# First norm's sum in a decoder trunk's expert stage: rows kept on chip, or spread by TensorE, with 20 or 22 initial expert places

## The reference

```python
x = _layer_norm(DEEPNORM_ALPHA * x + mixed, ln1_g[l], ln1_b[l])        # z * g + b
ffn = _hier_moe(x, ...)      # per expert e: silu(x Wg[e]) * (x Wu[e]), weighted, times Wd[e]
x = _layer_norm(DEEPNORM_ALPHA * x + ffn, ln2_g[l], ln2_b[l])
```

## Time and profile before

| | |
|---|---|
| median of 3 runs | 1338.53 us (1337.99 to 1340.18) |
| profiled execution, own time | 1340.83 us |
| its span, first to last instruction | 1338.6 us |
| busy share PE, DVE, ACT, POOL | 98%, 44%, 36%, 2% |
| TensorE clock granted, mean | 0.994 of full |
| DMA over the span | 364.95 MB, mean 273 GB/s |
| expert loads | 3 x 64 units of 1024 KB, median 21 to 23 us from issue to landing |

### The profile page before, as it was taken

How to read it: one execution, slowest core, us unless ns; L and a number is a source line. 1 busy time by engine, 2 the same in 40 slices (tenths; PEclk the granted TensorE clock), 3 DMA queues, 4 the chain that set the end, 5 groups by cost and what they waited for, 6 DMA issues and landing times.

```text
span 1338.6 us, 17749 instructions
## 1 busy us (share of the span) xinstructions
PE 1310.5 (98%) x7285; PEld 964.2 (72%) x7285; DVE 584.2 (44%) x757; ACT 483.3 (36%) x671; POOL 28.2 (2%) x49
## 2 busy tenths in 40 slices
PE   9999999999999999999999999999999999999994
PEld 9999989998888888888888888754444443544432
DVE  4387444446545655554555555515112121220206
ACT  4454444435465634454333433422111121211211
POOL 1000000400000000000100001000000000000000
PEclk9999999999999999999999999999999999999997
DMA  9767555545545445655566795799999999999995
GB/s 303 259 195 263 176 188 189 189 159 172 173 138 177 157 142 174 202 162 165 182 196 218 263 392 174 271 379 413 422 421 421 422 421 421 422 421 421 420 406 218
DMA packets 120461, 364.95 MB, mean 273 GB/s; under 512 B 11528, under 2 KB 17096, under 8 KB 96336
## 3 DMA queue, kind: packets, MB, share of 16 engines
q1 hardware_dynamic: 114080, 359.58, 72.3%
q10 hardware_dynamic: 6320, 4.49, 1.1%
HBM read 361.95 MB, written 2.10 MB: 272 GB/s over the span
## 4 chain that ended last, share of the span: by engine, by line
PE 91%; DMA 6%; DVE 2%; SPq 1%; ACT 0%; issue 0%; DVEq 0%
PE main L1127 19%; PE main L1129 19%; PE main L1128 19%; PE main L528 14%; PE att L599 7%; PE att L482 4%; DMA mraw<-in_expert_w_down_dram 3%; DMA mraw<-in_expert_w_up_dram 2%; PE att L1376 1%; DMA raw<-in_w_in_dram 1%; PE main L494 1%; PE main L495 1%; PE att L1359 1%; PE att L1395 1%; PE att L1391 1%; PE att L1346 0%
## 5 line engine op out<-in xcount | busy, mean ns | idle before, releaser
L1793 DVE TENSOR_TENSOR wlo<-raw,whi 128x2048 fp32r<-128x2048 f32 x134 | 308.1, 2299 | 353.9 <-ACT whi L1542 353.9
L1542 ACT ACTIVATE whi<-raw 128x2048 fp32r<-128x2048 f32 x134 | 256.1, 1912 | 413.3 <-PE main L1129 410.5
L528 PE MATMUL main<-mraw,xg 128*64 128x512 f32 x1024 | 225.2, 595 | 0.7 <-DMA mraw<-in_expert_w_up_dram 0.6
L1127 PE MATMUL main<-whi,xhi 128*128 128x512 f32 (+1 forms) x544 | 203.8, 375 | 0.0
L1129 PE MATMUL main<-whi,xlo 128*128 128x512 f32 (+1 forms) x544 | 201.7, 371 | 0.0
L1128 PE MATMUL main<-wlo,xhi 128*128 128x512 f32 (+1 forms) x544 | 201.5, 370 | 0.0
L528 PEld LDWEIGHTS main<-mraw,xg 128*64 128x64 f32 x1024 | 72.0, 137 | 136.7 <-issue 135.4
L1127 PE MATMUL main<-xhi,whi 128*128 128x256 f32 (+1 forms) x560 | 159.5, 285 | 0.9 <-DVE wlo L1925 0.5
L1128 PE MATMUL main<-xlo,whi 128*128 128x256 f32 (+1 forms) x560 | 158.4, 283 | 0.0
L1129 PE MATMUL main<-xhi,wlo 128*128 128x256 f32 (+1 forms) x560 | 158.4, 283 | 0.0
L1129 PEld LDWEIGHTS main<-whi,xlo 128*128 128x128 f32 x544 | 102.5, 188 | 17.7
(11 more groups left out here) (331 smaller groups left out, 1340.2 us busy)
## 6 DMA issues: line engine op xcount, KB each, us to landing
raw<-in_w_in_dram SPq DMA_DIRECT2D x95, 1024.0 KB, 5.0
mraw<-in_expert_w_gate_dram SPq DMA_DIRECT2D x64, 1024.0 KB, 21.6
mraw<-in_expert_w_up_dram SPq DMA_DIRECT2D x64, 1024.0 KB, 23.0
mraw<-in_expert_w_down_dram SPq DMA_DIRECT2D x64, 1024.0 KB, 21.1
raw<-in_w_branch_dram SPq DMA_DIRECT2D x24, 1024.0 KB, 5.1
raw<-in_w_out_dram SPq DMA_DIRECT2D x16, 1024.0 KB, 6.6
xin<-in_x_dram SPq DMA_DIRECT2D x4, 512.0 KB, 8.5
out_dram<-out_acc SPq DMA_DIRECT2D x8, 256.0 KB, 2.1
```

The source lines that it names most:

```text
L528: ins = pe.matmul(main[0][half, w, :], xg[:, k, half], src[:, kk * DE:(kk + 1) * DE], start=(k == 0), stop=(k == KT - 1))
L1127: pe.matmul(o, ah, bh, start=start, stop=False, skip_group_check=skip)
L1542: act.activation(whi[:, u % SPLIT, 0:n], raw[:, slot, 0:n], ACT.Copy).then_inc(hi_done, 1)
L1793: dve.tensor_tensor(wlo[:, u % SPLIT, 0:n], raw[:, slot, 0:n], whi[:, u % SPLIT, 0:n].bitcast(F32), ALU.subtract).then_inc(lo_done, 1)
```

## The change

Three things are changed together.

1. The broadcast rows `l1g` and `l1b` and their two loads are gone. `khT` and `qst` become initial places, so that `NP` is 22 and units 6 and 7 are loaded into them at the point of SP's list where the rows' loads stood, before the w_out weights.
2. Units and places are no longer the same number: `first` gives the place of each of the first 22 units. Units 8 and 9 go to places 14 and 15 (`late`), which so far held units 14 and 15, so that `out_acc` is free for the sum earlier. SP still issues by places, so these two go out after the units 10 to 17.
3. `g` and `b` stay as eight rows, in a tile of their own (`rows`), which ACT scales by ALPHA. PE **spreads** a row of 512 to 128 partitions by a matmul with a column of the identity, broadcast, as its weights. In pair 0, between the two halves of gate_up 2, four spreads put g into the four banks of `att`; DVE multiplies `z` by them (eight multiplies, before the gating), and PE's first down matmul waits for that (`acc_ok`). In pair 1, each of the eight scatters begins with a spread of b into the same bank, on which the scatter's matmuls then add.

```diff
+        rows = sb("rows", [P, 512])
-        l1g, l1b = at("l1g", made["khT"], [P, D]), at("l1b", made["qst"], [P, D])
...
+        norm_places = (len(places), len(places) + 1)
+        places += [made["khT"], made["qst"]]
         NP = len(places)
-        places += [made["khT"], made["qst"]]
+        late = [once[0], once[1]]
+        first = [0, 1, 2, 3, 4, 5, *norm_places, *late, *(j for j in range(6, router_place + 1) if j not in late)]
-        second_round = [j for j in range(NP) if j not in once]
-        GROWN = NP + len(second_round)
-        ring = second_round[:4] + [NP, NP + 1] + second_round[4:]
+        ring = [j for j in first if j not in once]
         def place(g):
-            if g < NP:
-                return g
-            return second_round[g - NP] if g < GROWN else ring[(g - GROWN) % MRAW]
+            return first[g] if g < NP else ring[(g - NP) % MRAW]
...
+            def spread(o, r):
+                return pe.matmul(o, ident[0:2 * QUADS, r:r + 1].to_broadcast([2 * QUADS, P]), gb, start=True,
+                                 stop=(r < QUADS), skip_group_check=True)
...
-                    pe.matmul(o, rows, yhi[:, c % 2, :], start=True, stop=False)
-                    pe.matmul(o, rows, ylo[:, c % 2, :], start=False, stop=True).then_inc(sc_ps, 1)
+                    if with_b:
+                        spread(o, QUADS + c)
+                    pe.matmul(o, place_t, yhi[:, c % 2, :], start=not with_b, stop=False, skip_group_check=with_b)
+                    pe.matmul(o, place_t, ylo[:, c % 2, :], start=False, stop=True, skip_group_check=with_b).then_inc(sc_ps, 1)
...
+                        if fixed == 0 and q == 2 and w == 1:
+                            pe.wait_ge(xg_out, 4)
+                            pe.wait_ge(gb_out, 2)
+                            for r in range(QUADS):
+                                spread(att[:, r, :], r).then_inc(l1_in, 1)
...
+                    if fixed == 0 and f == 0:
+                        pe.wait_ge(acc_ok, 1)
...
             def start_sum():
-                dve.wait_ge(m_used, once[1] + 1)
-                dve.wait_ge(l1_in, 32)
+                dve.wait_ge(m_used, first.index(late[1]) + 1)
                 dve.wait_ge(z_ok, T)
-                for t in range(T):
-                    for q in range(QUADS):
-                        cols = slice(q * 512, (q + 1) * 512)
-                        ins = dve.scalar_tensor_tensor(out_acc[:, t, cols].rearrange("p (m k) -> p m k", k=4),
-                                                       xr[:, t, cols].rearrange("p (k m) -> p m k", k=4), ALPHA,
-                                                       l1g[:, cols].rearrange("p (m k) -> p m k", k=4), ALU.mult, ALU.mult)
-                link(ins)
-                for t in range(T):
-                    ins = dve.scalar_tensor_tensor(out_acc[:, t, :], l1b[:], ALPHA, out_acc[:, t, :], ALU.mult, ALU.add)
+                for q in range(QUADS):
+                    cols = slice(q * 512, (q + 1) * 512)
+                    dve.wait_ge(l1_in, q + 1)
+                    for t in range(T):
+                        ins = dve.tensor_tensor(out_acc[:, t, cols].rearrange("p (m k) -> p m k", k=4),
+                                                xr[:, t, cols].rearrange("p (k m) -> p m k", k=4),
+                                                att[:, q, :].rearrange("p (m k) -> p m k", k=4), ALU.mult)
...
+                if starts:
+                    start_sum()
                 gated(m)
-                if first:
-                    start_sum()
-                else:
+                if not starts:
                     put_last(m - 1)
...
-            sp.dma_start(l1g[:], A["ln1_g"].to_broadcast([P, D])).then_inc(l1_in, 16)
-            sp.dma_start(l1b[:], A["ln1_b"].to_broadcast([P, D])).then_inc(l1_in, 16)
+            first_units(sp, norm_places)
...
+                    act.activation(gb, gb, ACT.Copy, scale=ALPHA).then_inc(gb_out, 1)
```

More of the change, by code:

```diff
@@ L245, in build @@
         places.append(made["sig"])
+        norm_places = (len(places), len(places) + 1)
+        places += [made["khT"], made["qst"]]
         NP = len(places)
-        places += [made["khT"], made["qst"]]
+        late = [once[0], once[1]]
+        first = [0, 1, 2, 3, 4, 5, *norm_places, *late, *(j for j in range(6, router_place + 1) if j not in late)]
         mraw = [at(f"mraw{j}", o, [P, UNIT]) for j, o in enumerate(places)]
-        second_round = [j for j in range(NP) if j not in once]
-        GROWN = NP + len(second_round)
-        ring = second_round[:4] + [NP, NP + 1] + second_round[4:]
+        ring = [j for j in first if j not in once]
         assert len(ring) == MRAW
         def place(g):
-            if g < NP:
-                return g
-            return second_round[g - NP] if g < GROWN else ring[(g - GROWN) % MRAW]
+            return first[g] if g < NP else ring[(g - NP) % MRAW]
         def user_before(g):
-            return max((e for e in range(g) if place(e) == place(g)), default=None)
-        LOOP0, LAST0 = (FIRST * MU - GROWN) % MRAW, (FIRST * MU + MU - GROWN) % MRAW
+            return max((e for e in range(g) if place(e) == place(g)))
+        LOOP0, LAST0 = (FIRST * MU - NP) % MRAW, (FIRST * MU + MU - NP) % MRAW
         L2R = MU - MRAW
@@ L290, in build @@
         sums, gbr = carve(1, "sums", [P, 2, NG + NE]), carve(1, "gbr", [P, 2, NG + NE])
-        gb, gbT = at("gb", made["cT"], [2 * QUADS, 512]), carve(1, "gbT", [P, 2 * KT])
+        gb, gbT = rows[0:2 * QUADS, :], carve(1, "gbT", [P, 2 * KT])
         wrg, wre = at("wrg", made["ddsa"], [P, KT, NG]), at("wre", made["dist"], [P, KT, NE])
@@ L395, in first_units @@
         def first_units(sp, some):
-            for r in some:
-                if r < 4:
+            for j in some:
+                if j < 4:
                     sp.wait_ge(unit_used, U1)
-                elif r < 6:
+                elif j < 6:
                     sp.wait_ge(m_ps, 8)
-                elif r < 6 + RAW:
-                    sp.wait_ge(lo_done, U1 + 11 + r - 6)
-                elif r == router_place:
+                elif j < 6 + RAW:
+                    sp.wait_ge(lo_done, U1 + 11 + j - 6)
+                elif j == router_place:
                     sp.wait_ge(r_ps, T)
-                else:
-                    sp.wait_ge(unit_used, U1 + 4 * QUADS - (1 if r < 8 + RAW else 0))
-                load_unit(sp, r, 0, r)
+                elif j < router_place:
+                    sp.wait_ge(unit_used, U1 + 4 * QUADS - (1 if j < 8 + RAW else 0))
+                load_unit(sp, first.index(j), 0, j)
         def moe_loads(sp):
-            first_units(sp, range(6, NP))
+            first_units(sp, range(6, router_place + 1))
             for g in range(NP, FIRST * MU):
[L412 to L415, removed]
+                sp.wait_ge(m_used, user_before(g) + 1)
                 load_unit(sp, g % MU, g // MU, place(g))
@@ L484, in gather, with scatter @@
                 ins.then_inc(xg_ps, 1)
-            def scatter(c, before):
+            def spread(o, r):
+                return pe.matmul(o, ident[0:2 * QUADS, r:r + 1].to_broadcast([2 * QUADS, P]), gb, start=True,
+                                 stop=(r < QUADS), skip_group_check=True)
+            def scatter(c, before, with_b=False):
                 pe.wait_ge(y_lo, before * 4 + c + 1)
@@ L534, in put @@
                     if fixed != 0:
-                        scatter(c, m - 1)
+                        scatter(c, m - 1, fixed == 1)
                 pe.wait_ge(hot_ok, 1 + m)
@@ L1517, in _ @@
                         for k in range(4):
-                            ins = pe.transpose(att[:, 2, k * 8:(k + 1) * 8], gb[:].rearrange("r (m k) -> r k m", k=4)[:, k, :],
+                            ins = pe.transpose(att[:, 2, k * 8:(k + 1) * 8], gb.rearrange("r (m k) -> r k m", k=4)[:, k, :],
                                                ident[0:2 * QUADS, 0:2 * QUADS])
```

4 lines of the change are left out of this document (2 added, 2 removed).

## The result

| | before | after |
|---|---|---|
| median (4 runs each, in one batch) | 1339.22 us (1337.99 to 1340.18) | 1352.53 us (1352.36 to 1352.87) |
| ratio | | 1.0100, 95% interval 1.0088 to 1.0112 |
| profiled execution, own time; span | 1340.83; 1338.6 | 1352.59; 1350.4 |
| TensorE clock granted, mean | 0.994 | 0.989 |

Slower by 13.3 us: the sign was forecast, the size was twice the 6.6 us of the sum, and the result lies 5 us above the range. Most of what follows is about the clock in the last row of the table.

A forecast was written before the change was run, and what follows sets the result against it. It took the DMA queue as the bound: the last unit's landing plus 22.7 us. PE's +8.7 us at unit 24 made unit 43 land 6.6 us later; 1338.5 + 6.6 = 1345.1 us, range 1339.5 to 1347.5.

The forecast's parts named there:

- the 6.6 us of the sum: Queue: unit 43 lands at 950.5 us instead of 943.9, so the whole kernel ends 6.6 us later.
- The sign, and what decides it: Whole kernel: slower, chance 0.81, because unit 43's load waits for PE to release unit 24 and the queue runs dry.
- 0.87 us a spread: PE, pairs 0 and 1: each spread is two fp32 instructions of about 0.435 us, 0.87 us together.
- Cheap spreads: Rival, PE: 0.218 us an instruction, ten spreads 4.4 us, total +0.1 to +2.3 us; chance 0.12.
- sum +8.7 at the release of unit 24: PE: four spreads in pair 0 (+3.5 us) and six in pair 1 (+5.2) delay unit 24's release by 8.7 us.
- Lands 7.05 us later: Queue near 943 us: unit 43, issued on a dry queue with another load following at once, takes 7.05 us to land.
- The other bound: Queue: a lone load on a dry queue takes 4.9 us; unit 43 would land at 948.3 us, +4.4.
- Two units early: 5.0 us: Queue after 920 us: two units less have to pass, 2 x 2.49 = 5.0 us gained if the queue never waits.
- The end set by the queue: Kernel's end: the last unit's landing plus 22.7 us of fixed work; the queue's +6.6 us exceeds PE's 4.3.
- a sign against itself: Last two pairs: PE without any wait for loads would make PE and not the queue the bound.
- Both sums: Kernel's end: the queue's sum, +6.6 us, and PE's alone, 10.4 us more work less 6.1 of waits, some 4.3.
- The sum on DVE: DVE, pair 0: eight multiplies, 8.6 us, end at 907.8 us before the gating with 4 us to spare; costs nothing.

The follow-up runs named there:

- f1: The changed kernel, unaltered, profiled once more on another chip; 1347.88 us beside 1339.75 for the kernel before, one execution of each.
- e3: The changed kernel with every spread on 128 rows, the tile rows zeroed below its first eight; 1346.11 us against 1338.82 for the kernel before.
- e4: The changed kernel without any spread, g and b left out of the sum, 22 initial places kept; 1336.92 us against 1338.82 for the kernel before.
- g1: The changed kernel, unaltered, timed again in one batch on one chip with g2; median 1352.61 us against 1339.69 for the kernel before.
- f3: The kernel of e3, unaltered, profiled once more on another chip; way from pair 0's first expert matmul to pair 1's 63.92 us, no total time given.
- g2: The kernel of e3, unaltered, timed in one batch on one chip with g1; median 1345.88 us, ratio to the kernel before 1.0031 to 1.0058.
- e1: The kernel before plus four unused matmuls on 8 rows where the change has pair 0's four spreads; 1343.21 us against 1338.82.
- e2: The kernel before plus four unused matmuls on 128 rows where the change has pair 0's four spreads; 1341.38 us against 1338.82.
- f2: The kernel of e8, unaltered, profiled once more on another chip; way from pair 0's first expert matmul to pair 1's 58.75 us, no total time given.
- e8: The changed kernel with only the 8-row spreads of g in pair 0, b left out of the sum; 1342.75 us against 1339.2 for the kernel before.

## Why the prediction had the sign right and the size wrong

- **The sign, and what decides it: right.** Unit 43 waits for unit 24 in both kernels, the queue runs dry near 903 and 940, and what PE loses before unit 24 reappears at the last landing, less what the load saves on a dry queue. From the start of pair 0 both moved by 13.6 and 13.8 us after, and by 6.8 and 7.4 in f1.
- **"0.87 us a spread": right for the spread itself.** 0.91 in pair 0, and +9.0 on the way in e3 for the +8.7 of the sum. Cheap spreads, the rival, did not occur.
- **The failed step: "sum +8.7 at the release of unit 24".** It priced each spread by its own duration and let the work behind it run as before. Measured at the issue of unit 43 it was +17.7: 9.0 of spreads, 2.0 more because a scatter's matmul starts 1.05 us after an 8-row spread's start and 0.56 after a 128-row one's, and 6.7 of four half-clock stretches. The prediction put the clock at nothing without a reason, though the trace of before had such a stretch (0.66 in the window 870 to 875). Its +6.6 is near what e3 (+7.3) and f1 (+8.1, one execution) took, and half of what seven executions of nine took.
- **"Lands 7.05 us later": too long.** On the dry queue unit 43 took 5.0 us after, 4.8 in f1, 4.7 in e3. The other bound, the lone load at 4.9, was right, though it was not the best of that trace, as the prediction has it: the load issued at 841.2 us landed after 4.7. What had been slow in units 20 and 21 was not the pairing. This took 2.1 us off and hid part of the first error. In f1 the landing of unit 43 is +6.8, for a forecast of +6.6, and that is luck: 11.1 - 4.3 where the sum had 8.7 - 2.1.
- **"Two units early: 5.0 us".** An upper bound, and said so ("if the queue never waits"); alone they brought 1.9 (e4).
- **The end set by the queue: only where few stretches or none follow the spreads.** After 1190 us PE still waits for loads for 1.3 us in f1 and g1 and for 1.4 to 2.4 us in e3, f3 and g2; in the profiled execution of the result it waits for none, which the prediction listed as a sign against itself. Both sums had grown to nearly the same size.
- **The sum on DVE: right.** 7.67 us, 7.5 us to spare; no wait of PE for it.

The Trainium skill, "TensorE: Matmul & The Clock Gate", Part 1, "What's actually happening", says that the clock depends on how busy the array has been of late, and that the number of slow matmuls at a kernel's start differs from run to run. g1 shows such a difference within the kernel: 0.994 and 0.987 for the same kernel on the same chip. The first must be read with care: in every window above between 900 and 950 us with a clock under 1.00, PE is busy 5.00 us of 5.00. Reading that rule by the busy share of the profile, one would expect no loss at all.

What stays open is why the 8 rows do it, and why not in every execution. e1 against e2 and g1 against g2 show that rows are what tells the kernels apart, with nothing changed but the other 120 rows, which hold zeros in g2 and data in e2. In what way the chip counts them was not measured, nor how many rows would be enough.

## What to carry to other kernels

A small matmul that uses a few of 128 partitions costs its full length on PE, and can cost nearly as much again in the work behind it (9.0 and 7.0 us on the way here). Pad its rows with zeros if the tile has room: here that is worth 6.4 us (e3) and 6.7 us (g2 beside g1) for one memset. Price PE work inserted into a stretch without gaps by what is released behind it, and compare the mean granted clock of several executions, not one, before the size of an effect is believed. Where a row is only copied, a rounded part and a remainder in one float32r matmul cost a third of the fp32 one (1.20 us against 3.69 for four).

## What the runs showed of the hardware

- The clock fell from 2.4 to 1.2 GHz for 3.4 us at a time, behind fp32 matmuls of 8 rows, with PE busy without a gap: five stretches in the profiled execution after, none between 880 and 990 us in the three profiles of the kernel with 128 rows. In f1, f2 and e8 none followed either, with the same 8-row spreads; these three had one before pair 0, and after, e1 and g1, where one followed, had not.
- An early stretch, between 864 and 871 us and ahead of the experts, stands in eight of the sixteen profiles. Pair 0 starts at 874.5 to 876.1 us in these, at 873.5 to 874.0 in the others.
- An fp32 matmul of 128 columns and 512 long takes 0.91 us on 8 rows and on 128 alike, in two instructions.
- A float32r matmul behind an fp32 spread starts 1.05 us after the spread's start if that has 8 rows (after, f1), 0.56 us if it has 128 (e3). For the matmuls of 64 columns behind the four spreads of pair 0 it makes no difference (3.62 and 3.63 us).
- A 1 MB load on a dry queue landed 4.7 to 5.0 us after its issue (after, f1, e3; before, at 823.3 us, 4.9); on the full queue the rate is 421 GB/s before and after.
